# Block products over ten of sixteen feature tiles: 640-column weight blocks held in both chunks of a pair

## What is computed

```python
# block one (sliding-window attention with sinks)
h = rmsnorm(x, g_pre)
o, z = swa_sink_mixer(h, w_in_a, sinks_a)
y = (o * silu(z)) @ w_out_a
x = x + rmsnorm(y, g_post)
# block two, layers l = 0 and 1 (latent attention, short convolution, memory attention)
y = concatenate([a_out, c_out, m_out], axis=-1) * silu(gate)
o = y @ w_o[l]
x = x + rmsnorm_2(o, post_norm_g[l])
```

## Time and profile before

| what | value |
|---|---|
| median of three runs | 2198.35 us (2197.67 to 2198.75) |
| the profiled execution | 2198.36 us |
| its span, first to last instruction | 2196.4 us |
| TensorE busy | 2178.9 us (99%) |
| VectorE, ScalarE, GpSimd busy | 1516.4, 837.9, 267.3 us |
| mean granted TensorE clock | 0.999 |
| first pairs, layers 0 and 1, start | 510.3 and 1285.1 us |

### The profile page before, as it was taken

The page is one execution under the profiler, slowest core; times in us unless marked ns, Lnnn a source line. Parts: engine busy times, 40 slices in busy tenths (PEclk is TensorE's granted clock), DMA queues, the critical chain, the costliest instruction groups (busy, mean ns, idle before and its releaser), DMA issues.

```text
span 2196.4 us, 27828 instructions
## 1 busy us (share of the span) xinstructions
PE 2178.9 (99%) x10428; PEld 1819.7 (83%) x10428; DVE 1516.4 (69%) x2184; ACT 837.9 (38%) x1307; POOL 267.3 (12%) x255
## 2 busy tenths in 40 slices
PE   8999999999999999999999999999999999999998
PEld 7888888888888888888888888888888888888887
DVE  6677788888978643567677778786434677677665
ACT  6433433453345421334333533454213443435221
POOL 0100000116720100000000067201000000000000
PEclk9999999999999999999999999999999999999999
DMA  7445545442267222225443422573222154434532
GB/s 282 168 156 154 159 156 162 144 151 94 81 215 270 87 96 97 75 73 156 138 144 115 143 96 96 190 271 114 96 95 75 65 158 132 143 118 154 176 118 108
DMA packets 91018, 303.24 MB, mean 138 GB/s; under 512 B 7536, under 2 KB 48752, under 8 KB 67888
## 3 DMA queue, kind: packets, MB, share of 16 engines
q1 hardware_dynamic: 84912, 275.00, 38.0%
q10 hardware_dynamic: 4896, 17.30, 2.1%
q0 software_dynamic: 1120, 9.70, 1.2%
HBM read 253.74 MB, written 48.23 MB: 137 GB/s over the span
## 4 chain that ended last, share of the span: by engine, by line
PE 96%; POOL 1%; DVE 1%; DMA 1%; issue 1%; ACT 0%; SPq 0%; DVEq 0%; POOLq 0%; ACTq 0%
PE acc L657 67%; PE sc L657 12%; PE ov L657 6%; PE sc L881 2%; PE sc L882 1%; PE ov L821 1%; PE sc L808 1%; PE sc L807 1%; PE sc L1064 1%; PE sc L1063 1%; DMA raw<-w_dram 0%; DMA g<-xT_dram 0%; PE acc L673 0%; PE acc L676 0%; PE acc L672 0%
## 5 line engine op out<-in xcount | busy, mean ns | idle before, releaser
L657 PE MATMUL acc<-h_all,hi 128*128 128x512 f32 x4160 | 1287.8, 391 | 8.3 <-DVE h_all L1717 8.3
L657 PEld LDWEIGHTS acc<-h_all,hi 128*128 128x128 f32 x4160 | 776.0, 188 | 169.4 <-issue 11.4
L657 PE MATMUL acc<-h_all,lo 128*128 128x512 f32 x2080 | 810.6, 390 | 0.0
L1625 DVE TENSOR_TENSOR lo<-raw,hi 128x2048 fp32r<-128x2048 f32 (+3 forms) x158 | 345.2, 2185 | 172.8 <-ACT hi L1173 170.9
L657 PEld LDWEIGHTS acc<-h_all,lo 128*128 128x128 f32 x2080 | 391.0, 188 | 82.0
L1173 ACT ACTIVATE hi<-raw 128x2048 fp32r<-128x2048 f32 (+3 forms) x158 | 289.1, 1830 | 431.3 <-PE acc L657 263.4
L1255 ACT ACTIVATE prob<-prob,st 128x256 f32<-128x256 f32 x128 | 63.6, 498 | 109.4 <-DVE st L1778 109.4
L657 PE MATMUL sc<-hi,h_all 128*128 128x512 f32 (+1 forms) x320 | 90.9, 369 | 0.0
L1332 ACT ACTIVATE hi<-raw 128x512 fp32r<-128x512 f32 x50 | 30.2, 626 | 114.3 <-PE sc L882 95.8
L657 PEld LDWEIGHTS sc<-hi,h_all 128*128 128x128 f32 x320 | 58.1, 189 | 10.5 <-issue 0.5
L555 POOL TENSOR_TENSOR t_raw<-g 128x512 f32<-128x512 f32 x4 | 5.2, 1290 | 484.8 <-DVE lo L1625 484.8
(11 more groups left out here) (331 smaller groups left out, 3468.5 us busy)
## 6 DMA issues: line engine op xcount, KB each, us to landing
raw<-w_dram SPq DMA_DIRECT2D x170, 1024.0 KB, 4.9
turned<-pt SPq DMA_DIRECT2D x32, 512.0 KB, 3.2
pt<-turned SPq DMA_DIRECT2D x64, 256.0 KB, 5.0
turned<-pt SPq DMA_DIRECT2D x32, 448.0 KB, 3.0
pt<-turned SPq DMA_DIRECT2D x64, 224.0 KB, 3.9
xr<-residual ACTq DMA_DIRECT2D x16, 512.0 KB, 5.2
residual<-g ACTq DMA_DIRECT2D x16, 512.0 KB, 4.7
raw<-w_dram SPq DMA_DIRECT2D x8, 896.0 KB, 6.6
```

Of the source, the lines that this page charges most:

```text
L657: ins = pe.matmul(to, a, b, start=first and n == 0, stop=last and n == 2)
L1625: dve.tensor_tensor(lo[c.slot][:, 0:width], raw[c.slot][:, 0:width], hi[c.slot][:, 0:width].bitcast(F32), ALU.subtract).then_inc(lo_done, 1)
```

## The change

The block scheme covers ten feature tiles, 8 to 15 and 6, 7 (`BLOCK_TILES`). A block has 640 columns and a block product five steps. Chunk c now holds the first output tile's two blocks (`LEFT`, `RIGHT`) and its plain rest of six tiles (`REST`, 768 columns), chunk d the same of the second output tile. S1 is therefore the sum of two blocks of d. The plain parts are `rest_product`, 18 matmuls each. GpSimd makes four more token sums of 128x256 (`last_turned_sums`), with copies and subtractions of their own (`t5_hi`, `t5_lo`), and product 2 of the first pair waits for them as well. The `hi` of d's rest moves to the start of ScalarE's part, and the `hi` of c's rest (`second`) comes between the wait for S2 and the copy of S2. The angle steps are dealt out anew: one of the three subtractions in each of the pairs q = 3, 4, 5, the phase in q = 6, and the five last ones behind chunk 15.

```diff
-    SU, TW, TILES = 512, 2048, S // 2
+    NK, TW, TILES = 5, 2048, S // 2
+    SU, BLOCK_TILES = NK * P, tuple(range(KT // 2, KT)) + (6, 7)
...
+        t5_at = (g0 + (KT - 2) * 4 * S, a0 + 12288)
+        t5_parts, t5_raw = ([sb(f"{n}{i}", 2 * S, dt, at=t5_at[i]) for i in range(2)] for n, dt in (("t5_parts", F32R), ("t5_raw", F32)))
...
+        LEFT, RIGHT, REST = slice(0, SU), slice(SU, 2 * SU), slice(2 * SU, CW)
...
+            def last_turned_sums(l):
...
+                done = l * 12 + 8
...
             def weight_sums(l, q):
                 c, d, no = pair_of(l, q)
-                w, s2, s1 = raw[c.slot], s_two[:, 0:SU], s_two[:, SU:2 * SU]
+                one, two, s2, s1 = raw[c.slot], raw[d.slot], s_two[:, 0:SU], s_two[:, SU:2 * SU]
+                pool.wait_ge(loaded[d.slot], (d.uses + 1) * 16)
+                if q > Q0:
+                    pool.wait_ge(unit_lo, (no - 1) * 5 + 3)
+                pool.tensor_tensor(s1, two[:, LEFT], two[:, RIGHT], ALU.add).then_inc(s_sum, 1)
                 pool.wait_ge(loaded[c.slot], (c.uses + 1) * 16)
-                if q > Q0:
-                    pool.wait_ge(unit_lo, (no - 1) * 6 + 3)
-                pool.tensor_tensor(s1, w[:, A21], w[:, A22], ALU.add).then_inc(s_sum, 1)
                 pool.wait_ge(s_sum, no * 4 + 1)
-                pool.tensor_tensor(s2, s1, w[:, A11], ALU.subtract).then_inc(s_sum, 1)
-                pool.tensor_tensor(w[:, A21], w[:, A11], w[:, A21], ALU.subtract).then_inc(s_sum, 1)
+                pool.tensor_tensor(s2, s1, one[:, LEFT], ALU.subtract).then_inc(s_sum, 1)
+                pool.tensor_tensor(two[:, LEFT], one[:, LEFT], two[:, LEFT], ALU.subtract).then_inc(s_sum, 1)
             def last_weight_sum(l, q):
                 c, d, no = pair_of(l, q)
...
+                one = raw[c.slot]
                 pool.wait_ge(s_sum, no * 4 + 3)
-                pool.wait_ge(unit_lo, no * 6 + 1)
-                pool.tensor_tensor(w[:, A11], w[:, A12], s_two[:, 0:SU], ALU.subtract).then_inc(s_sum, 1)
+                pool.wait_ge(unit_lo, no * 5 + 1)
+                pool.tensor_tensor(one[:, LEFT], one[:, RIGHT], s_two[:, 0:SU], ALU.subtract).then_inc(s_sum, 1)
...
                 turned_sums(l, 1)
+                last_turned_sums(l)
...
+                for m in range(NK):
                     both = src(m)
-                    w = slice(unit.start + m * P, unit.start + (m + 1) * P)
...
+                    w = slice(part.start + m * P, part.start + (m + 1) * P)
+                    high_, low_, end = hi[c.slot][:, w], lo[c.slot][:, w], last and m == NK - 1
                     pe.matmul(bank(bank_).rearrange("p (s n) -> p s n", s=2), high_, both, start=first and m == 0, stop=end, skip_group_check=True)
                     ins = pe.matmul(bank(bank_, TILES), low_, both[:, 0, :], start=False, stop=end, skip_group_check=True)
...
+                pe.wait_ge(unit_lo, no * 5 + 1)
                 if q > Q0:
                     pe.wait_ge(folded, no * 7 - 2)
-                block_product(c, 1, UNIT[0], y_block(0, 0), True, False).then_inc(product_done, 1)
-                pe.wait_ge(unit_lo, no * 6 + 2)
-                pe.wait_ge(t_low, l * 4 + 4)
+                block_product(c, LEFT, 1, y_block(0, 0), True, False).then_inc(product_done, 1)
+                pe.wait_ge(unit_lo, no * 5 + 2)
+                pe.wait_ge(t_low, l * 5 + 5)
                 if q > Q0:
                     pe.wait_ge(folded, no * 7)
-                block_product(c, 2, UNIT[1], t_block(1), True, False).then_inc(product_done, 1)
-                pe.wait_ge(unit_lo, no * 6 + 3)
-                block_product(c, 3, UNIT[2], t_block(0), True, False).then_inc(product_done, 1)
+                block_product(d, LEFT, 2, t_block(1), True, False).then_inc(product_done, 1)
+                pe.wait_ge(unit_lo, no * 5 + 3)
+                block_product(c, RIGHT, 3, t_block(0), True, False).then_inc(product_done, 1)
                 pe.wait_ge(half_lo, no + 1)
                 pe.wait_ge(evacuated[c.slot], c.accs)
-                half_product(d, 0, acc[c.slot][:, :]).then_inc(half_done, 1)
-                pe.wait_ge(unit_lo, no * 6 + 4)
+                rest_product(c, acc[c.slot][:, :]).then_inc(half_done, 1)
+                pe.wait_ge(unit_lo, no * 5 + 4)
                 pe.wait_ge(folded, no * 7 + 2)
-                block_product(c, 2, UNIT[3], t_block(2), False, False).then_inc(product_done, 1)
-                pe.wait_ge(unit_lo, no * 6 + 6)
+                block_product(d, RIGHT, 2, t_block(2), False, False).then_inc(product_done, 1)
+                pe.wait_ge(lo_done, c.n + 1)
                 pe.wait_ge(folded, no * 7 + 3)
-                block_product(c, 1, UNIT[2], y_block(1, 0), False, True).then_inc(product_done, 1)
-                block_product(c, 3, UNIT[0], y_block(1, 1), False, True).then_inc(product_done, 1)
-                pe.wait_ge(lo_done, c.n + 1)
+                block_product(c, RIGHT, 1, y_block(1, 0), False, True).then_inc(product_done, 1)
+                pe.wait_ge(unit_lo, no * 5 + 5)
+                block_product(c, LEFT, 3, y_block(1, 1), False, True).then_inc(product_done, 1)
+                pe.wait_ge(lo_done, d.n + 1)
...
+            def first_units(l, q, second):
                 c, d, no = pair_of(l, q)
...
                 act.wait_ge(loaded[c.slot], (c.uses + 1) * 16)
                 if q > Q0:
                     act.wait_ge(product_done, (no - 1) * 6 + 6)
                 else:
                     act.wait_ge(chunk_done, c.n - 1)
-                unit_high(c, UNIT[0], w[:, A11], unit_hi)
-                act.wait_ge(chunk_done, c.n - 1)
+                unit_high(c, LEFT, raw[c.slot][:, LEFT], unit_hi)
                 act.wait_ge(s_sum, no * 4 + 2)
-                unit_high(c, UNIT[1], s_two[:, 0:SU], unit_hi)
-                unit_high(c, UNIT[2], s_two[:, SU:2 * SU], unit_hi)
+                second()
+                act.wait_ge(chunk_done, d.n - 2 if q > Q0 else d.n - 1)
+                unit_high(d, LEFT, s_two[:, 0:SU], unit_hi)
+                unit_high(c, RIGHT, s_two[:, SU:2 * SU], unit_hi)
                 act.wait_ge(s_sum, no * 4 + 3)
-                unit_high(c, UNIT[3], w[:, A21], unit_hi)
+                unit_high(d, RIGHT, raw[d.slot][:, LEFT], unit_hi)
             def first_half(l, q):
                 c, d, no = pair_of(l, q)
-                act.wait_ge(loaded[d.slot], (d.uses + 1) * 16)
+                act.wait_ge(loaded[c.slot], (c.uses + 1) * 16)
                 if q > Q0:
                     act.wait_ge(half_done, no)
                 else:
-                    act.wait_ge(chunk_done, d.n - 1)
-                act.activation(hi[d.slot][:, HALF[0]], raw[d.slot][:, HALF[0]], ACT.Copy).then_inc(half_hi, 1)
+                    act.wait_ge(chunk_done, c.n - 1)
+                unit_high(c, REST, raw[c.slot][:, REST], half_hi)
...
+                act.wait_ge(chunk_done, d.n - 1)
+                unit_high(d, REST, raw[d.slot][:, REST], half_hi)
                 act.wait_ge(s_sum, no * 4 + 4)
                 act.wait_ge(product_done, no * 6 + 1)
-                unit_high(c, UNIT[0], w[:, A11], unit_hi)
+                unit_high(c, LEFT, raw[c.slot][:, LEFT], unit_hi)
                 if q > Q0:
                     for t in (2 * q - 2, 2 * q - 1):
...
                 act.wait_ge(product_done, no * 6 + 3)
-                unit_high(c, UNIT[2], w[:, A12], unit_hi)
-                unit_high(c, UNIT[1], w[:, A22], hi_done)
-                act.wait_ge(chunk_done, d.n - 1)
-                act.activation(hi[d.slot][:, HALF[1]], raw[d.slot][:, HALF[1]], ACT.Copy).then_inc(hi_done, 1)
+                unit_high(c, RIGHT, raw[c.slot][:, RIGHT], hi_done)
+                unit_high(d, LEFT, raw[d.slot][:, RIGHT], hi_done)
...
+                def first_tiles():
+                    first_half(l, Q0)
+                    output_tile(l, 2, 0, chunk2(l, WO + 2), None)
+                    for m in range(2, 4):
+                        t_hi(l, m)
+                    t5_hi(l)
+                first_units(l, Q0, first_tiles)
...
                 if q == 2:
                     angle_turns()
                 elif q == 3:
-                    angle_less_turns()
+                    angle_less_turns((TURN_A,))
                 elif q == 4:
-                    angle_within(ALU.is_gt, PI, -TWO_PI)
+                    angle_less_turns((TURN_B,))
                 elif q == 5:
-                    angle_within(ALU.is_lt, -PI, TWO_PI)
+                    angle_less_turns((TURN_C,))
                 elif q == 6:
-                    angle_end()
...
+                    angle_phase()
...
-                unit_low(c, UNIT[0], w[:, A11], no * 6 + 5, unit_lo)
+                dve.wait_ge(unit_hi, no * 5 + 5)
+                unit_low(c, LEFT, raw[c.slot][:, LEFT]).then_inc(unit_lo, 1)
                 dve.wait_ge(product_done, no * 6 + 3)
                 fold(p15[:, :], 3)
```

(27 more changed lines are left out.)

110 lines of the change are left out of this document (54 added, 56 removed).

## The result

Five runs of the changed kernel have a median of 2239.85 us (2237.0 to 2243.4); beside them the kernel before has 2198.55. The ratio is 1.0186, 95% interval 1.0175 to 1.0197: **41 us slower**. The forecast was 2224 us, slower with 0.91; the direction was right, the time lies 4 us above the range of 2205 to 2236. The profiled execution took 2243.41 us, its span 2241.6 us; it is the slowest of the five, 3.6 us over their median.

The account below looks back on a forecast made before the run. The prediction took TensorE, busy 99% of the span, as the bound. Its terms, -2.6 - 1.8 + 9.0 + 20.4 + 0.5 + 0.7 = +26.2 us on 2198.36, gave 2224 us, range 2205 to 2236.

Parts of the forecast that it names:

- TensorE's saving: TensorE's work per pair falls from 20.77 to 20.51 us, saving 2.6 us over ten pairs.
- The rival of another pace: Five-step products issue at another pace than 0.3525 us a step; 0.02 us more gives 2231 us; chance 0.03.
- The angle: In layer 0's second pair the fold comes in time, so a 1.8 us stall goes.
- the 0.7 us for the moved operations: Five angle operations behind chunk 15 delay the memory tiles' preparation on VectorE: 0.7 us lost, between 0 and 3.
- The opening: Product 2 of each layer's first pair waits for S2, held up by d's landing: 4.5 us, 9.0 in all.
- with each 1024-column subtraction and GpSimd's sums one behind the other it is about 516.6: Layer 0's opening: the time S2 is ready with these conflicts, against 515.2 without any.
- by a third: Opening: stretch of GpSimd's sums, as 1.62 for 1.28 us, assumed for the wait's upper end of 6.5 us.
- The round: Loop from d's landing to its next, through GpSimd, ScalarE, VectorE and load: 23.6 us, 3.1 over TensorE's pair, q = 4 to 6.
- the variant: VectorE and GpSimd block each other for whole instructions, fixes keep their length: 3.3 us of collisions, 2227 us; chance 0.3 within 0.72.
- q = 3 ... 0.9 us: Pair q = 3 still lives on the opening's wait and earlier room, so loses only 0.9 us per layer.
- the loop is longer still: Rival: landings of 7.5 us, full collisions and a late fold holding products come together, 2241 us; chance 0.06.
- The chance of faster: Rival: everything stays hidden, with S2's `lo` and token parts ready by 512.1 and loop under 20.5, 2194.0 us; chance 0.05, faster 0.03.

Follow-up runs that it names:

- e3: Changed kernel with S1 made from chunk c's blocks, so S1 and S2 no longer wait for d's landing (sums not the reference's): 2210.3 us, ratio 1.0047.
- e9: Changed kernel with d loaded ahead of c from the second pair on, and the splits on ScalarE and VectorE reordered to suit: 2217.1 us, ratio 1.0082.
- e13: Changed kernel with loads swapped, opening reordered, and c's rest ahead of S2 on ScalarE and VectorE: 2200.87 us, ratio 1.0004 to the kernel before.
- e1: Kernel before the change with only the new order of the angle operations: 2198.61 us, ratio 0.9996 (0.9987 to 1.0005).
- e5: Changed kernel with 26 extra matmuls filling the wait behind product 1 of each layer's first pair: 2238.97 us, ratio 1.0181.
- e14: e13 with the opening reordered again: weight sums before first squares, tiles 2 and 3 after the sums' highs, first angle operations earlier: 2199.85 us, ratio 1.0002.
- e6: Changed kernel with GpSimd's three late fixes of a pair ahead of the next pair's weight sums: 2237.43 us, ratio 1.0173.
- e7: Changed kernel with e6's edit, plus c's rest and the final additions reordered around S2 and d's load on ScalarE and VectorE: 2241.95 us, ratio 1.0194.
- e2: Changed kernel with GpSimd's two later groups of token sums ahead of the weight sums and first squares: 2234.05 us, ratio 1.0155.

## Why the prediction was right, and where wrong

- **TensorE's saving**: forecast 20.51 us for a pair, 2.6 in all; measured 20.57 where nothing waits (e3, e9, e13), so 2.2 us in ten pairs. Right. The rival of another pace falls.
- **The angle**: right on the stall (1.6 us in e1), and unmeasurable in the time. No run shows the 0.7 us for the moved operations; e1's 0.8 us against before is within its interval.
- **The opening**, "4.5 us ... 9.0 us in all": right in place and chain, too small. The wait was 6.3 and 6.6 us. The step of the sum that failed is "with each 1024-column subtraction and GpSimd's sums one behind the other it is about 516.6": I let the collisions cost 1.4 us in all. GpSimd's chain alone lost 3.0 us by the rows: S3 0.6, the squares 0.7, two sums of 256 columns 0.84 each; and S2's `lo` stands behind all token parts, as forecast. (Landing of d and start of the pair were both 1.1 to 1.2 us later than forecast, which cancels.) These are readings of rows; no run takes the opening's collisions away alone. The Trainium skill ("SBUF — State Buffer", section "SBUF: two separate sides") has the other engine blocked for the whole instruction, so a short sum can double: 0.74 to 1.58 agrees, where I had scaled "by a third". On top came the clock, 1.4 and 2.9 us (e5), which had no term. The first pairs are 8.1 and 9.5 us over 20.57.
- **The round**, "23.6 us, 3.1 over": the mechanism is shown by e3 and e9; the size was 24.4. It was 3.3 for S1 and S2 (forecast 3.2), 1.5 for ScalarE (1.5), 12.2 for VectorE with its collisions (12.0), 7.3 for the load (6.9). GpSimd's fixes did not stay as long as they were, as the variant had it: 1.32 us in place of 0.74. Each pair q = 4, 5, 6 then pays 3.4 to 4.4, where the forecast had 3.1; the clock's dips at 567.6 and 1390.2 are among it.
- **"q = 3 ... 0.9 us"** failed: 3.0 us in layer 0, 1.7 in layer 1. The opening left no room, since VectorE, late with S2, was late with d: d's load went out 18.5 us into the first pair. In layer 0 the first two angle operations, 2.3 us, stand ahead of the load too.
- **Sum.** Opening 17.6 us in place of 9.0, pairs q = 3 to 6 28.0 in place of 20.4 + 0.5, saving and angle 3.8 in place of 4.4; 41.8 in the pairs of the traced run. The traced runs differ by 45 us in all and the medians by 41.3, so this isn't a sum of the medians' difference. The larger part of the miss is the opening: 3.9 us more of waits in the two layers and 4.3 us of clock that stood at nothing. Two chains were found and each was taken inside its bounds, and the range left out the high end where both are long; that late sums bring collisions, waits and clock falls at once is my reading and not tested. The forecast's own rival "the loop is longer still", 2241 us at 0.06, was nearest in its number, and in its mechanism only in part: the load needed 7.3 and not 7.5 us, the collisions in the loop 3.0 and not 3.9, no product waited for a fold, and the opening lost 17.6 where it had 13. That its number fits is luck in part.
- **The chance of faster**, 0.03: the condition "GpSimd makes up 4.5 us in the opening, and the loop is under 20.5" was the right one; e13 and e14 come near it (their longest waits in layer 1's opening are 1.3 and 1.0 us) and reach no difference, not 2194.

Open: what of the round's 12.2 us on VectorE is collisions other than those with the late fixes (e6: 1 us a pair); how much of the opening's waits the collisions cost; and whether the clock costs anything in the medians.

## To carry to other kernels

When a change moves an operand from one load to the next, walk the whole round from that landing back to the issue of the same buffer's next load. If it is longer than the bottleneck's period by anything, each iteration pays the difference, and cutting work on the bottleneck gains nothing. Let the operand that starts the longest chain land first, and let nothing on its queue that waits for the bottleneck stand ahead of it.

## What the runs showed of the hardware that I had not expected

- The granted clock fell to 0.50 at 516.4 for 6.8 us and at 1311.7 for 10.2 us, in waits of 6.3 and 6.6 us, and for 3.4 us in or just behind some waits of about 2 us, but not others of the same length (e7, waits of 2.19 us each: at 544.6 and 592.4, not at 569.0 and 616.9). The length alone does not tell: a wait of 1.82 us at 566.7 in e5 was followed by a fall, one of 3.23 us at 539.0 in e2 was not. The Trainium skill ("TensorE: Matmul & The Clock Gate", section "Why this matters for your kernels") warns of idle gaps between bursts; the trace agrees for the waits of 6.3 and 6.6 us.
- Two loads of 1 MB: the second lands 6.5 to 7.9 us behind its issue when issued 1.3 us behind the first (changed kernel, both layers), and in most pairs 4.8 to 4.9 us when issued 2.6 us behind (e9). By these figures the gap was worth 2.3 us of the round and the order 1.7.
- An operation of 0.74 us on GpSimd took 1.58 beside VectorE's subtractions, and VectorE's `lo` of 0.82 took 1.35 beside GpSimd's fixes.
